# Weights rounded three units ahead before the eviction of the present unit, and norm steps one unit earlier, in a two-block transformer kernel

## The chip, the cores and the metric

The kernel runs on one core of a Trainium2 chip. The metric is the time of one execution on the device in microseconds. Three runs of the kernel before gave 3142.19 (median), 3136.18 and 3153.81 us.

## What is computed

A sequence of 256 tokens with 1024 features passes two blocks of two layers each. Everything is fp32.

The first block, per layer: a projection `x @ w_in` whose parts feed a sliding-window attention, a gated short convolution and a block attention; the three results are projected, weighted with sigmoid gates and summed; then a residual sum with a layer norm, a SwiGLU network and a second residual sum with a layer norm:

```python
x = layer_norm(ALPHA * x + mix, ln1_g[l], ln1_b[l])
ffn = swiglu(x, w_ffn_gate[l], w_ffn_up[l], w_ffn_down[l])   # hidden size 2816
x = layer_norm(ALPHA * x + ffn, ln2_g[l], ln2_b[l])
```

The second block has two streams, the latents `h` (256 tokens, from the first block) and a context `hc` (256 tokens). Each layer modulates them by a vector `mod = silu(c) @ w_ada[l] + b_ada[l]`:

```python
h = h + 0.5 * gt1 * swiglu_2(ada_norm(h, g_ffn1[l], sh1, sc1), w1_ffn1[l], w3_ffn1[l], w2_ffn1[l])
u = ada_norm(h, g_mix[l], sh2, sc2)        # rms_norm(h, g) * (1 + scale) + shift
# convolution, latent attention and Fourier mixing of u @ w_in[l], merged by gates
h = h + gt2 * y
h = h + 0.5 * gt3 * swiglu_2(ada_norm(h, g_ffn2[l], sh3, sc3), w1_ffn2[l], w3_ffn2[l], w2_ffn2[l])
```

and the same for `hc`, except that its last updates in the second layer aren't needed.

## The kernel before, in words

Features lie on the 128 partitions, tokens in the free dimension; `h` holds context in columns 0 to 255 and latents in 256 to 511. All weight matrices are cut into *units*, tiles of up to eight 128x128 blocks (kt blocks, 512 KB where kt is 8), 850 in all, stored one behind the other in the order of use. Every product is computed as three fp32r products: weights and inputs are split into a rounded high part and a remainder, and TensorE adds high x high, high x low and low x high (lines 1767 to 1769; 1711 to 1713 where two units are interleaved). A full unit has 24 such products, on 256 or on 512 columns.

Each unit passes a chain over four slots (`SLOTS = 4`): SP loads it into `raw` (line 434), ACT rounds it into `whi` (`high`, line 521), DVE computes the remainder `wlo` (`low`, line 990), TensorE multiplies, and ACT or DVE takes the result out of one of four PSUM banks (the eviction, `evac`). Semaphores tie the steps: `unit_high_ready`, `unit_low_ready`, and `unit_used`, which TensorE raises at the end of a unit. SP loads unit u+4 when `low(u)` is done; `high(u)` waits for its load and for unit u-4 to be used, since it overwrites that slot. Weights are split three units ahead (`AHEAD = 3`).

Each engine has its own program, written out in order, and runs it in that order. The program goes by stages, named after what is computed: qkv0, bbb0, gate0, merge0, out0, up00, down00, up01 ... for the first block (block number left out, the first digit is the layer), then fup100c, fdown100c, fup100 ... for the second (f1 and f2 are the two SwiGLU networks, a final c means context columns). `stream` runs a stage: for each unit j it calls the eviction of unit j, `high` (on ACT) or `low` (on DVE) of unit j+3, and then, if given, a step of something else, `then(j)`. Where `then` is missing a hardware loop runs over four or twelve units. The stages qkv, bbb, gate, mix, kv and q have loops of their own, in which `high` and `low` already stand in front.

In an up stage (`hidden`) units alternate between gate and up matrix. For even j ACT evicts with SiLU (line 607); for odd j DVE multiplies (line 1166), ACT rounds the product (610) and DVE computes its remainder (1023). In a down stage DVE evicts by adding to the residual (lines 1305, 1308 or 1428).

Beside the up and down stages DVE also computes the modulation vector: one 512 KB tile of `w_ada` after another, loaded through POOL's queue (493), multiplied and summed with `silu(c)` (line 1054). The table `BESIDE` says how many such tiles go with four units of a stage.

The norms of the second block lie beside the stages around them. For one stream a norm has these steps: squares on ACT (638) and their sum on DVE (1223), a sum over features by a small matmul on PE (`by_token`, 1733), the square root on ACT (642, with a table load on each side where SiLU is in use), the reciprocal and a diagonal matrix on DVE (1232, 1177), a matmul with ones that spreads it over the partitions (`spread`, 1752), and then for each of the eight tiles `half_apply` on DVE (1245), `half_shift` on ACT (648) and `half_low` on DVE (1251). A `Follow` record says behind which unit each step stands: the sum, the root, the inverse, the spread, and for each unit the tiles. `DOWN` is used in the down stage whose other stream is just being computed, `UP` in fup200c and fup110c, `INTO` in mix0, `INTO_LAST` in mix1. `seam` runs the two halves of a down stage, with the norm of the first half beside the second.

The layer norms of the first block (`norm1`) stand between stages and TensorE waits for them.

## Time and profile before

| | us |
|---|---|
| median of three runs (lowest, highest) | 3142.19 (3136.18, 3153.81) |
| profiled execution | 3141.47 |
| its span, first to last instruction | 3139.8 |
| TensorE matmuls busy | 2978.0 (95%) |
| VectorE (DVE) busy | 2075.6 (66%) |
| ScalarE (ACT) busy | 1367.1 (44%) |
| mean granted TensorE clock | 0.977 |

The span is nearly the whole execution. Matmuls overlap and the profiler models their ends, so TensorE's busy share is not a share of its peak; the time from the start of one matmul to the start of the next tells its pace. Idle time of DVE and ACT costs nothing where TensorE doesn't wait for them. The clock is given as a share of 2.4 GHz; 0.5 is the lower level, 1.2 GHz.

### The profile page before, as it was taken

How to read it: one execution, taken by the hardware profiler on the slowest of the kernel's cores; microseconds unless marked ns; L12 is line 12 of the kernel's file. 1: busy time of each engine (PE TensorE's matmuls, PEld its weight loads, DVE VectorE, ACT ScalarE, POOL GpSimd, SP SyncE). 2: the span in 40 equal slices, each digit the busy share in tenths (PEclk: the TensorE clock that was granted, in tenths of full speed). 3: DMA queues.
4: the chain of work that ended last, by engine and by line, in shares of the span. 5: the costliest groups of instructions: out<-in, count | busy, mean ns of one | idle time of the engine just before them, and what ended most of it. 6: DMA issues, size and time to landing. Idle time of an engine off the chain costs nothing.

```text
span 3139.8 us, 52114 instructions
## 1 busy us (share of the span) xinstructions
PE 2978.0 (95%) x19700; PEld 2677.8 (85%) x19700; DVE 2075.6 (66%) x3359; ACT 1367.1 (44%) x2222; POOL 76.6 (2%) x149
## 2 busy tenths in 40 slices
PE   8998998998999999999889999999999999889898
PEld 8888998887999988897568888888998889769898
DVE  4657785557777777778843366767767667775655
ACT  4555444454545432354542254222542225654443
POOL 0000000000000000000000000100001000000000
PEclk9999999998999999999999999999999999999999
DMA  6435664434665565551102344544545445215454
GB/s 230 139 104 168 227 233 162 139 104 160 202 211 180 187 215 190 176 177 61 57 29 92 98 168 154 194 156 172 185 145 198 151 147 169 90 54 188 154 186 141
DMA packets 147696, 486.16 MB, mean 155 GB/s; under 512 B 16320, under 2 KB 25792, under 8 KB 147392
## 3 DMA queue, kind: packets, MB, share of 16 engines
q1 hardware_dynamic: 126640, 407.22, 38.5%
q0 software_dynamic: 20880, 76.56, 7.1%
q8 instruction: 115, 1.88, 0.2%
q14 instruction: 61, 0.50, 0.0%
HBM read 482.66 MB, written 1.05 MB: 154 GB/s over the span
## 4 chain that ended last, share of the span: by engine, by line
PE 78%; DVE 11%; ACT 5%; issue 4%; DMA 1%; DVEq 0%; ACTq 0%; SPq 0%; POOLq 0%
PE bank L1767 22%; PE bank L1769 21%; PE bank L1768 21%; DVE wlo L990 4%; ACT whi L521 3%; PE bank L1711 2%; PE bank L1712 2%; PE bank L1713 2%; DVE acc L1515 1%; DMA bbb<-in_w_ada 1%; PE bank L1984 1%; PE bank L1842 1%; DVE bbb L1054 1%; PE aux L1968 1%; DVE big L1245 1%
## 5 line engine op out<-in xcount | busy, mean ns | idle before, releaser
L990 DVE TENSOR_TENSOR wlo<-raw,whi 128x1024 fp32r<-128x1024 f32 (+4 forms) x850 | 948.2, 1116 | 482.1 <-ACT whi L521 479.6
L1767 PE MATMUL bank<-uhi,whi 128*128 128x256 f32 (+1 forms) x4000 | 1250.2, 313 | 16.5 <-DVE wlo L990 9.8
L1768 PE MATMUL bank<-ulo,whi 128*128 128x256 f32 (+1 forms) x4000 | 1237.7, 309 | 0.0
L1769 PE MATMUL bank<-uhi,wlo 128*128 128x256 f32 (+1 forms) x4000 | 1237.6, 309 | 0.0
L521 ACT CAST whi<-raw 128x1024 fp32r<-128x1024 f32 (+4 forms) x850 | 805.9, 961 | 271.1 <-PE bank L1769 170.3
L1767 PEld LDWEIGHTS bank<-uhi,whi 128*128 128x128 f32 x4000 | 757.2, 189 | 79.8 <-issue 22.5
L1768 PEld LDWEIGHTS bank<-ulo,whi 128*128 128x128 f32 x4000 | 757.5, 189 | 44.8 <-issue 0.2
L1769 PEld LDWEIGHTS bank<-uhi,wlo 128*128 128x128 f32 x4000 | 757.3, 189 | 44.6
L1767 PE MATMUL bank<-yhi,whi 128*128 128x256 f32 (+1 forms) x1432 | 444.5, 310 | 21.3 <-DVE wlo L990 14.7
L1768 PE MATMUL bank<-ylo,whi 128*128 128x256 f32 (+1 forms) x1448 | 445.7, 308 | 0.0
L1769 PE MATMUL bank<-yhi,wlo 128*128 128x256 f32 (+1 forms) x1432 | 440.1, 307 | 0.0
L1767 PEld LDWEIGHTS bank<-yhi,whi 128*128 128x128 f32 x1432 | 272.9, 191 | 41.4 <-DVE wlo L990 14.7
L1768 PEld LDWEIGHTS bank<-ylo,whi 128*128 128x128 f32 x1448 | 275.9, 191 | 14.6
L1769 PEld LDWEIGHTS bank<-yhi,wlo 128*128 128x128 f32 x1432 | 272.6, 190 | 14.3
L610 ACT CAST yhi<-pp 128x256 fp32r<-128x256 f32 (+3 forms) x108 | 53.7, 498 | 355.0 <-DVE pp L1166 355.0
L1054 DVE CUSTOM_DVE_ANT_0 acc<-big,cs 128x1024 f32<-128x1024 f32 x128 | 156.4, 1222 | 20.7 <-DMA big<-in_w_ada 18.9
L1428 DVE SCALAR_TENSOR_TENSOR h<-bank,hgt,h 128x256 f32<-128x256 f32 x168 | 77.4, 480 | 100.7 <-PE bank L1769 76.0
L607 ACT ACTIVATE pp<-bank 128x256 f32<-128x256 f32 (+1 forms) x108 | 51.1, 473 | 210.0 <-PE bank L1769 205.9
L1711 PE MATMUL bank<-uhi,whi 128*128 128x256 f32 x288 | 90.0, 312 | 46.4 <-DVE ulo L1023 29.1
L1054 DVE CUSTOM_DVE_ANT_0 acc<-vt,cs 128x1024 f32<-128x1024 f32 x102 | 124.6, 1222 | 2.2
L1166 DVE TENSOR_TENSOR pp<-pp,bank 128x256 f32<-128x256 f32 (+1 forms) x108 | 57.5, 533 | 99.4 <-PE bank L1769 99.3
L960 ACT ACTIVATE pp<-bank,par 128x512 f32<-128x512 f32 (+1 forms) x48 | 27.9, 582 | 198.0 <-PE bank L1769 198.0
(265 smaller groups left out, 2922.2 us busy)
## 6 DMA issues: line engine op xcount, KB each, us to landing
raw<-in_w_stream SPq DMA_DIRECT2D x674, 512.0 KB, 3.4
big<-in_w_ada POOLq DMA_DIRECT2D x64, 512.0 KB, 3.8
vt<-in_w_ada POOLq DMA_DIRECT2D x51, 512.0 KB, 3.7
raw<-in_w_stream SPq DMA_DIRECT2D x80, 256.0 KB, 2.7
raw<-in_w_stream SPq DMA_DIRECT2D x48, 384.0 KB, 3.1
bbb<-in_w_ada POOLq DMA_DIRECT2D x29, 512.0 KB, 3.7
raw<-in_w_stream SPq DMA_DIRECT2D x32, 192.0 KB, 2.3
raw<-in_w_stream SPq DMA_DIRECT2D x16, 128.0 KB, 2.0
```

Of the source, the lines that this page charges most:

```text
L521: sc.copy(whi[:, u % SLOTS, 0:n], raw[:, u % SLOTS, 0:n]).then_inc(s_high, 1)
L610: sc.copy(ht[:, 2 * i + (tile + k), c0:c1], hid(k)[:, c0:c1]).then_inc(s_ahi, 1)
L990: ve.tensor_tensor(wlo[:, u % SLOTS, 0:n], raw[:, u % SLOTS, 0:n], whi[:, u % SLOTS, 0:n].bitcast(F32), ALU.subtract).then_inc(s_low, 1)
L1054: ve.tensor_tensor_reduce(out_, ring(name)[r], cs[:, s, :].rearrange("p (a b) -> p a b", a=out_.shape[1]), 1.0, 0.0, ALU.mult, ALU.add, su ...
L1166: ve.tensor_tensor(hid(k)[:, c0:c1], sg(k)[:, c0:c1], bank(u0, j)[:, c0:c1], ALU.mult).then_inc(read(u0, j), 1)
L1428: ins = ve.scalar_tensor_tensor(h[:, m, cols], bank(u0, j)[:, cols], gate(m, s), h[:, m, cols], ALU.mult, ALU.add)
L1711: te.matmul(out_, whi[:, s, w], hi(k)[:, c0:c1], start=k == 0, stop=False)
L1712: te.matmul(out_, whi[:, s, w], lo(k)[:, c0:c1], start=False, stop=False)
L1713: ins = te.matmul(out_, wlo[:, s, w], hi(k)[:, c0:c1], start=False, stop=k == n - 1)
L1767: te.matmul(out_, whi[:, u % SLOTS, w], hi(k)[:, c0:c1], start=k == 0, stop=False)
L1768: te.matmul(out_, whi[:, u % SLOTS, w], lo(k)[:, c0:c1], start=False, stop=False)
L1769: ins = te.matmul(out_, wlo[:, u % SLOTS, w], hi(k)[:, c0:c1], start=False, stop=k == plan.kt[u] - 1)
```

## The change

Two things change. In `stream` on ACT and DVE, `high` and `low` of unit j+3 now stand in front of the eviction of unit j instead of behind it, in the loop as in the written-out parts. And three `Follow` records get other numbers: in `UP` and `INTO` the sum and the root stand behind unit 2 instead of 3 and the spread behind unit 4 instead of 5; in `UP` the inverse stands behind unit 3 instead of 4 and the tiles begin behind unit 4 instead of 5, one per unit; in `INTO_LAST` the inverse moves from 2 to 3 and the tiles from units 4 to 7 (two each) to units 5 to 7 (two, three, three). `DOWN` is as it was.

```diff
-UP = Follow(3, 3, 4, 5, {5: [0], 6: [1], 7: [2], 8: [3], 9: [4], 10: [5], 11: [6, 7]})
-INTO = Follow(3, 3, 3, 5, {5: [0], 6: [1], 7: [2], 8: [3], 9: [4], 10: [5], 11: [6, 7]})
-INTO_LAST = Follow(2, 2, 2, 4, {4: [0, 1], 5: [2, 3], 6: [4, 5], 7: [6, 7]})
+UP = Follow(2, 2, 3, 4, {4: [0], 5: [1], 6: [2], 7: [3], 8: [4], 9: [5], 10: [6], 11: [7]})
+INTO = Follow(2, 2, 3, 4, {5: [0], 6: [1], 7: [2], 8: [3], 9: [4], 10: [5], 11: [6, 7]})
+INTO_LAST = Follow(2, 2, 3, 4, {5: [0, 1], 6: [2, 3, 4], 7: [5, 6, 7]})
...
                 if then is not None:
                     for j in range(n):
+                        high(u0 + j + AHEAD)
                         evac(j % per, j // per)
-                        high(u0 + j + AHEAD)
                         then(j)
                     return
 
                 def body(i):
                     for j in range(per):
+                        high(u0 + j + AHEAD, i, per)
                         evac(j, i)
-                        high(u0 + j + AHEAD, i, per)
 
                 repeat(act, iters - 1, body, tallies)
                 for j in range(per):
+                    high(u0 + n - per + j + AHEAD)
                     evac(j, iters - 1)
-                    high(u0 + n - per + j + AHEAD)
...
```

The same three moves are made with `low` in `stream` on DVE.

The first place is DVE behind the loop of stage up00. L990 is the remainder of a weight unit, L1054 the sum over a tile of `w_ada` (its second row reads the sum), L1166 the product of an odd unit and L1023 its remainder. Before:

```order
L201 COMPARE_AND_BRANCH
L1054 ISA bbb,ada_sums<-bbb,cs 128x1024 [waits ada_sums_ready,ada_modulation_ready,ada_landed0]
L1054 ISA ada_sums 128x1
L990 TENSOR_TENSOR wlo<-raw,whi 128x1024 [waits unit_high_ready]
L1166 TENSOR_TENSOR lg<-lg,bank 128x256 [waits unit_used,bank_read2]
L1023 TENSOR_TENSOR ylo<-lg,yhi 128x256 [waits act_high_ready]
L990 TENSOR_TENSOR wlo<-raw,whi 128x1024 [waits unit_high_ready]
```

and now:

```order
L201 COMPARE_AND_BRANCH
L990 TENSOR_TENSOR wlo<-raw,whi 128x1024 [waits unit_high_ready]
L1054 ISA bbb,ada_sums<-bbb,cs 128x1024 [waits ada_sums_ready,ada_modulation_ready,ada_landed0]
L1054 ISA ada_sums 128x1
L990 TENSOR_TENSOR wlo<-raw,whi 128x1024 [waits unit_high_ready]
L1166 TENSOR_TENSOR lg<-lg,bank 128x256 [waits unit_used,bank_read2]
L1023 TENSOR_TENSOR ylo<-lg,yhi 128x256 [waits act_high_ready]
L990 TENSOR_TENSOR wlo<-raw,whi 128x1024 [waits unit_high_ready]
```

L990 has moved in front of L1054 with its wait for the tile of `w_ada`, and in front of L1166 and L1023; the order among the others is as it was.

The second place is DVE behind the sixth unit (j = 5) of stage fdown202, a seam with a norm. L1428 is the eviction, L1223 adds a square, L1245 applies the norm to a tile, L1251 computes a tile's remainder. Before:

```order
L1428 SCALAR_TENSOR_TENSOR h<-bank,hgt,h 128x256 [waits unit_used]
L990 TENSOR_TENSOR wlo<-raw,whi 128x1024 [waits unit_high_ready]
L1223 TENSOR_TENSOR big<-big 128x256 [waits norm_squares_ready,dve_step]
L1245 SCALAR_TENSOR_TENSOR big<-h,scl,aux 128x256 x2
L1251 SCALAR_TENSOR_TENSOR ulo<-big,mod,uhi 128x256 [waits half_high_ready]
```

and now:

```order
L990 TENSOR_TENSOR wlo<-raw,whi 128x1024 [waits unit_high_ready]
L1428 SCALAR_TENSOR_TENSOR h<-bank,hgt,h 128x256 [waits unit_used]
L1223 TENSOR_TENSOR big<-big 128x256 [waits norm_squares_ready,dve_step]
L1245 SCALAR_TENSOR_TENSOR big<-h,scl,aux 128x256 x2
L1251 SCALAR_TENSOR_TENSOR ulo<-big,mod,uhi 128x256 [waits half_high_ready]
```

L1428 has moved from the front of the row to the place between L990 and L1223.

The third place is ACT in stage fup110c, behind the second unit. L521 is the rounding of a weight unit, L607 SiLU of an even unit, L610 the rounding of an odd unit's product, L782 and L785 the table loads around the square root L642, L648 the shift of a norm tile. Before:

```order
L521 CAST whi<-raw 128x1024 [waits unit_used,unit_landed1]
L610 CAST yhi<-pp 128x256 [waits bank_read3]
L521 CAST whi<-raw 128x1024 [waits unit_used,unit_landed2]
L782 ACT_TABLE_LOAD
L642 ACTIVATE tok<-aux,cst 128x2 [waits sum_ready]
L785 ACT_TABLE_LOAD
L607 ACTIVATE pp<-bank 128x256 [waits unit_used]
L521 CAST whi<-raw 128x1024 [waits unit_used,unit_landed3]
L610 CAST yhi<-pp 128x256 [waits bank_read1]
L521 CAST whi<-raw 128x1024 [waits unit_used,unit_landed0]
L648 ACTIVATE uhi<-big,mod 128x256 [waits half_applied]
```

and now:

```order
L521 CAST whi<-raw 128x1024 [waits unit_used,unit_landed1]
L607 ACTIVATE pp<-bank 128x256 [waits unit_used]
L782 ACT_TABLE_LOAD
L642 ACTIVATE tok<-aux,cst 128x2 [waits sum_ready]
L785 ACT_TABLE_LOAD
L521 CAST whi<-raw 128x1024 [waits unit_used,unit_landed2]
L610 CAST yhi<-pp 128x256 [waits bank_read3]
L521 CAST whi<-raw 128x1024 [waits unit_used,unit_landed3]
L607 ACTIVATE pp<-bank 128x256 [waits unit_used]
L648 ACTIVATE uhi<-big,mod 128x256 [waits half_applied]
L521 CAST whi<-raw 128x1024 [waits unit_used,unit_landed0]
```

Each L521 stands in front of its L607 or L610. The square root with its two table loads now stands behind the SiLU of unit 2 and in front of the rounding that goes with unit 3, and the first L648 follows one unit sooner.

## Rows read from the trace of the kernel before

**Rows 1.** Page, part 1: busy time, share of the span, instructions.

```profile
PE 2978.0 (95%) x19700; PEld 2677.8 (85%) x19700; DVE 2075.6 (66%) x3359; ACT 1367.1 (44%) x2222; POOL 76.6 (2%) x149
```

**Rows 2.** Page, part 5: L990; idle time and its releaser come last.

```profile
L990 DVE TENSOR_TENSOR wlo<-raw,whi 128x1024 fp32r<-128x1024 f32 (+4 forms) x850 | 948.2, 1116 | 482.1 <-ACT whi L521 479.6
```

**Rows 3.** Waits by total: sum us, times, longest us.

```profile
PE bank L1711 <- DVE ulo L1023: 29.1, 6, 10.7
```

**Rows 4.** Windows: us; PE, PEld, DVE, ACT, POOL busy (count); clock, DMA share, GB/s.

```profile
1226.00:1315.60 89.60, 89.60 (x385) 72.05 (x384) 66.28 (x98) 23.31 (x30) 8.41 (x16) 1.00 0.53 190
297.90:340.30 42.40, 40.94 (x339) 40.08 (x338) 30.27 (x44) 19.07 (x30) 1.58 (x3) 1.00 0.57 198
363.10:410.30 47.20, 46.24 (x385) 45.62 (x385) 39.81 (x62) 19.55 (x30) 3.16 (x6) 1.00 0.66 233
787.10:828.10 41.00, 39.99 (x335) 39.53 (x334) 30.83 (x46) 18.68 (x29) 1.71 (x4) 1.00 0.60 207
850.90:898.50 47.60, 46.41 (x388) 45.81 (x389) 32.88 (x50) 21.11 (x32) 1.58 (x3) 1.00 0.57 198
1058.50:1101.70 43.20, 40.87 (x338) 40.05 (x338) 30.40 (x46) 19.03 (x30) 1.58 (x3) 1.00 0.58 196
```

**Rows 5.** Timeline of DVE in stage fup100: start us, busy us, instruction, [idle before].

```profile
1067.97 1.23 DVE L990 TENSOR_TENSOR wlo<-raw,whi 128x1024 fp32r<-128x1024 f32 x1 [0.31 <-ACT whi L521]
1071.36 1.22 DVE L1054 CUSTOM_DVE_ANT_0 acc<-big,cs 128x1024 f32<-128x1024 f32 x1 [2.16 <-DMA big<-in_w_ada]
...
1072.51 1.22 DVE L990 TENSOR_TENSOR wlo<-raw,whi 128x1024 fp32r<-128x1024 f32 x1
...
1085.55 0.08 DVE L1054 DVE_READ_ACCUMULATOR2_ANT ada_sums<- 128x1 f32 x1
1085.55 1.22 DVE L990 TENSOR_TENSOR wlo<-raw,whi 128x1024 fp32r<-128x1024 f32 x1
```

**Rows 6.** Timeline of DVE at the end of stage fdown202.

```profile
2252.94 1.23 DVE L990 TENSOR_TENSOR wlo<-raw,whi 128x1024 fp32r<-128x1024 f32 x1 [0.73 <-ACT whi L521]
2254.09 0.42 DVE L1223 TENSOR_TENSOR big<-big 128x256 f32<-128x256 f32 x1
2254.42 0.47 DVE L1245 SCALAR_TENSOR_TENSOR big<-h,scl,aux 128x256 f32<-128x256 f32 x1
2255.61 0.48 DVE L1428 SCALAR_TENSOR_TENSOR h<-bank,hgt,h 128x256 f32<-128x256 f32 x1
2256.42 1.22 DVE L990 TENSOR_TENSOR wlo<-raw,whi 128x1024 fp32r<-128x1024 f32 x1 [0.33 <-ACT whi L521]
```

**Rows 7.** Timeline of ACT, the same stretch, and one table load in fup110c.

```profile
2254.93 0.51 ACT L648 ACTIVATE uhi<-big,mod 128x256 fp32r<-128x256 f32 x1 [1.70 <-DVE big L1245]
2255.35 1.04 ACT L521 CAST whi<-raw 128x1024 fp32r<-128x1024 f32 x1
...
2269.08 1.28 ACT L782 ACT_TABLE_LOAD   x1
```

**Rows 8.** Timeline of DVE in the second half of stage fup110c.

```profile
2291.84 0.42 DVE L1166 TENSOR_TENSOR pp<-pp,bank 128x256 f32<-128x256 f32 x1
2292.73 0.43 DVE L1023 TENSOR_TENSOR ylo<-pp,yhi 128x256 fp32r<-128x256 f32 x1 [0.47 <-ACT yhi L610]
```

**Rows 9.** Timeline of PE in fup110c: the ones-matmul and its wait.

```profile
2275.11 1.22 PE L1752 MATMUL aux<-pp,cst 128*128 128x256 f32 x2 [2.89 <-DVE pp L1177]
```

**Rows 10.** Windows of the same seventh unit in fup110c and in fup200c.

```profile
2273.50:2281.40 7.90, 6.29 (x28) 6.11 (x29) 3.90 (x7) 1.88 (x4) 0.00 (x0) 0.57 0.38 135
1887.00:1893.60 6.60, 3.70 (x30) 3.53 (x29) 4.10 (x7) 2.76 (x5) 0.00 (x0) 1.00 0.35 132
```

**Rows 11.** Timeline of DVE at the end of stage out0.

```profile
277.58 1.22 DVE L990 TENSOR_TENSOR wlo<-raw,whi 128x1024 fp32r<-128x1024 f32 x1
```

**Rows 12.** Timeline of DVE in stage merge0, one period apart.

```profile
241.78 0.69 DVE L990 TENSOR_TENSOR wlo<-raw,whi 128x512 fp32r<-128x512 f32 x1
246.60 0.69 DVE L990 TENSOR_TENSOR wlo<-raw,whi 128x512 fp32r<-128x512 f32 x1
```

6 lines of the change are left out of this document (3 added, 3 removed).

## Prediction, written before the changed kernel ran

> **What bounds the kernel now.** I read the page's busy shares first, then its costliest groups, then the waits, then windows over single stages, and last the timelines of DVE and ACT at the seams between stages. TensorE is busy for 95% of the span, 2978 of 3139.8 us [rows 1], so an edit that only reorders ACT and DVE can win at most the roughly 160 us in which TensorE stands, and what it stretches. The largest idle time elsewhere is DVE's, 479.6 us before L990, the remainder of a weight unit, waiting for L521, the rounding on ACT [rows 2]. That total says nothing by itself: the question is where L990 or a norm step is the last thing TensorE waits for.
>
> A stage that loses nothing gives the measure. In fup102 16 units of 24 products each on 512 columns take 89.6 us [rows 4], 0.117 us per 256 columns, so a full unit on 256 columns needs 2.81 us. Against that: up00 takes 42.4 us for 14 units (39.4 needed), up01 47.2 for 16 (45.0), up10 41.0 for 14, up11 47.6 for 16, fup100 43.2 for 14 [rows 4]. The losses are 3.0, 2.2, 1.6, 2.6 and 3.8 us, 13.2 together. All stages on 512 columns stand like fup102 and cannot gain. The other losses sit at seams, where TensorE waits for normalized tiles (29.1 us in six waits for L1023 alone [rows 3]) and for the small ones-matmul of a norm [rows 9].
>
> **The change part by part.** No instruction is added or removed; the DMAs are the same, in the same order on SP's and POOL's queues. Since SP issues the load of unit u+4 when L990 of unit u is done, loads start earlier wherever L990 does, without more bytes.
>
> A. *Rounding and remainder ahead of the eviction, in the middle of a stage.* Unit j+3's L521 needs only that unit j-1 is used, while the eviction of unit j needs unit j itself. So each L990 moves ahead of one eviction and, in the stages with modulation work, of one L1054. In fup100 DVE waits 2.16 us for a modulation tile in front of L1054, and L990, behind it in the queue, comes at 1072.51; the next such point is at 1085.55 [rows 5]. That is 13.0 us for four units for which TensorE needs 11.3, so DVE's queue, stretched by the transfer, is the slower one, and it stays so: the change shortens no period, it puts one L990 more ahead of each stall. Worked through for up00, L990 comes 0.9 to 3.5 us earlier and takes away about 1.8 of the 3.0 us. For the three stages with one tile per four units (3.0+1.6+3.8 = 8.4) I take 5.0. In up01 and up11 there are two tiles per four units and DVE has no DMA wait but too much work: the lead with which the stage begins is used up at its end. L990 of every other unit moves ahead of a multiplication, a wait, a remainder and an L1054, some 2.6 us (0.42 + 0.47 + 0.43 + 1.22, durations as in [rows 5, 8]), which is more than each of these losses: I take 4.5 of 4.8. With up02 and up12 (half a microsecond) A gives 10.0; bounds 3 (only the starts gain) and 14 (all of it).
>
> B. *Ends of stages.* After the last unit of out0 L990, 1.22 us [rows 11], stands between the last residual sum and the centring that DVE does next. It moves into the time in which TensorE computes that unit. The centring must still wait for the ones-matmul, so only 0.35 us is won, three times (up00, qkv1, up10): 1.0. Before fup210 the same instruction stands ahead of the last square sum: 0.9. At the ends of bm0 and bm1 it stands in front of the eight remainders of u: 1.1 each. Sum 4.1, bounds 2 and 6.
>
> C. *merge0 and merge1.* L990 recurs after 4.82 us for three units [rows 12] that TensorE needs 4.2 for; DVE's own chain of three remainders, three products, two sums, a wait for ACT and one more remainder is the bound, and the cycle is the same in both orders. Only the start and the one stall at the second gating are displaced: 1.0 each, 2.0; bounds 0 and 4.
>
> D. *The seams with a norm (fdown100c, fdown102, bout0, fdown202, fdown112c).* Here the edit works against itself. ACT and DVE hand work to each other: L521, L990 1.07 us later, L1223 1.15 later, L1245 0.33 later, L648 on ACT 0.51 later, and 0.42 later the next L521 [rows 6, 7]; 3.48 us with one tile, more than the 2.81 of TensorE. L1428, the eviction (0.48 busy, 0.40 to the next start, since an instruction begins 0.08 before its forerunner ends), stands at 2255.61, in the part in which DVE would otherwise wait for ACT [rows 6]. It is free there. After the change it stands between L990 and L1223, inside the ring. Five rounds cost 2.0 us; the first tile comes 1.0 to 1.15 earlier, since L990 no longer sits between its eviction and L1245. Net the last tile comes 1.0 us later, and TensorE already waits for it. Loss 4 x 1.0 + 0.85 = 4.9; bounds 0 and 7.
>
> E. *UP, one unit earlier (fup200c, fup110c).* The square root and its two table loads of 1.28 us [rows 7] move from behind unit 3 to behind unit 2, the inverse to unit 3, the ones-matmul to behind unit 4. It gets there 2.8 us sooner, but its operand only 1.5 to 2.2 us sooner, because the inverse now stands behind an eviction, its copy and its remainder, so its wait grows from 2.89 [rows 9] to about 3.5 us. The tiles start one unit earlier and need one round fewer at the end; but on odd units L1245 now stands behind L1166 and L1023, 0.89 us apart [rows 8], which before ran beside ACT's rounding. A pair of units goes from 7.2 to 7.55 us. All told each first pair of fup200l and fup110l ends 0.35 us later beyond D: loss 0.7.
> The granted clock matters here. After the same wait the seventh unit's window has a clock of 0.57 in fup110c, 1.00 in fup200c; TensorE is busy for 6.29 us in the one and 3.70 in the other [rows 10], 2.6 us for half the clock (1.2 instead of 2.4 GHz). I leave one such stretch in two, as before: 0, bounds +2.6 and -2.6.
> The Trainium skill, "TensorE: Matmul & The Clock Gate", section "Part 1: The HAM clock gate", says that the gate's timing is not tied to the kernel, so the same program meets it differently from run to run; these rows agree, one wait of two having paid. By that rule the value taken stands; by the rows alone both waits, now longer, might pay, which is the third rival's price.
>
> F. *INTO and INTO_LAST.* In mix0 TensorE doesn't wait for the steps that move: 0. In mix1 the last step now holds three tiles instead of two and the one before it three as well; each tile costs about 0.4 on ACT and 0.8 on DVE: the context pair ends 1.2 us later. Bounds 0 and 1.7.
>
> Sum: 10.0 + 4.1 + 2.0 - 4.9 - 0.7 - 1.2 = 9.3 us less. The profiled execution took 3141.5 us (span 3139.8 and 1.7 around it), the median of the runs is 3142.2, so both stand together: 3132 in the profile, 3133 as a median.
>
> **The rivals.** *The seams don't pay and the stalls go entirely (faster).* If the eviction in D lies beside something after all and one more L990 ahead absorbs every modulation stall: 13.7 + 4.1 + 4 + 2.6 for the half clock = 24, so 3118. For it: leads at full lie near 6 us where DVE isn't late. Against it: 13.0 against 11.3 us per four units [rows 5].
> *Nothing measurable.* TensorE at 95% [rows 1] and gains at one end given back at the next: a unit ready earlier only waits in its slot. A at its lower bound of 3 with B 4.1 and C 2 against D to F 6.8 gives 2.3: 3140.
> *The seams win (slower).* The handshake of D with L1428 inside is the one place where TensorE surely waits. If A stays at 3 and B at 2, while the waits for the ones-matmul both fall into half clock (2.6 more) and D reaches 7: 3 + 2 - 7 - 2.6 - 0.7 - 1.7 = 7 slower, 3149. It decides from the point where a round costs more than 3.9 us. For it: the ring is already 3.48 us against 2.81. Against: A is five stages of clear, late L990.
>
> **How the numbers follow.** Forecast 3133: 0.45. Faster rival 3118: 0.25. Nothing: 0.18. Slower: 0.12. A measurement of this kernel can tell about 0.5%, 15.7 us. Below 3126.5 lies the faster rival and a fifth of the forecast: 0.34. Above 3157.9 lies the tail of the slower one: 0.07. The rest, 0.59, is within. The bounds of A to F reach from 3112 to 3150; the range 3115 to 3146 leaves one case in five out. The forecast's own range is 3125 to 3139.
>
> **What would show it.** A: in the windows of up00, up01, up10, up11 and fup100, shifted to where these stages then lie, 1 us or less lost in the two-tile stages, 1 to 2 in the others; L1054's DMA wait still there, L990 ahead of it. B: L1183 starts some 0.3 us closer to the last L1305. D: at the end of fdown202 L1428 between L990 and L1223, rounds of 3.9 us, TensorE's waits for L1023 larger by 1 us each. E: the wait before L1752 in fup110c about 3.5 us. The prediction is wrong if a round at the seams is no longer than 3.5 us, if the up stages keep their losses, or if the share of half clock (mean clock 0.977) moves by more than 0.003.

## The result and the profile after

The changed kernel takes 3150.32 us (median of 16 runs, 3145.22 to 3157.07) against 3143.31 (16 runs) of the kernel before on the same chip: ratio 1.0028, 95% interval 1.0018 to 1.0037. The prediction was 3133, range 3115 to 3146. By the ratio it is slower by about 8.8 us (the medians differ by 7.0) where 9.3 us less was forecast.

TensorE does the same work for the same time; what changed is where the others wait. Page, parts 1 and 5, after:

```profile
PE 2978.5 (95%) x19700; PEld 2678.1 (85%) x19700; DVE 2077.7 (66%) x3359; ACT 1374.2 (44%) x2222; POOL 76.6 (2%) x149
...
L990 DVE TENSOR_TENSOR wlo<-raw,whi 128x1024 fp32r<-128x1024 f32 (+4 forms) x850 | 948.4, 1117 | 565.7 <-ACT whi L521 558.9
```

DVE's wait for ACT before L990 rose from 479.6 [rows 2] to 558.9 us. Again the total alone says nothing. The windows of the five up stages do (the same units as in [rows 4], where they now lie: up00, up01, up10, up11, fup100):

```profile
295.70:336.10 40.40, 40.16 (x336) 39.68 (x335) 28.71 (x43) 17.01 (x27) 1.58 (x3) 1.00 0.61 208
361.40:406.40 45.00, 45.00 (x386) 45.00 (x386) 37.28 (x58) 18.93 (x29) 3.17 (x6) 1.00 0.66 232
783.30:823.10 39.80, 39.80 (x336) 39.32 (x334) 28.18 (x43) 16.64 (x26) 1.58 (x3) 1.00 0.62 211
848.70:894.20 45.50, 45.50 (x388) 45.50 (x389) 30.73 (x47) 19.79 (x29) 1.58 (x3) 1.00 0.57 197
1061.10:1104.30 43.20, 40.69 (x336) 39.87 (x334) 28.93 (x43) 17.59 (x27) 1.58 (x3) 1.00 0.57 195
```

In these windows the change did much of what it should: 42.4, 47.2, 41.0, 47.6 and 43.2 us became 40.4, 45.0, 39.8, 45.5 and 43.2, 7.5 us less, and TensorE stands still in up01 no more; fup100 alone gained nothing. But what comes behind the last unit of each stage is another matter. DVE at the end of up00, in the kernel before (start us, busy us, instruction, idle before it):

```profile
333.97 1.23 DVE L1054 CUSTOM_DVE_ANT_0 bbb<-bbb,cs 128x1024 f32<-128x1024 f32 x1
335.12 1.22 DVE L990 TENSOR_TENSOR wlo<-raw,whi 128x1024 fp32r<-128x1024 f32 x1
...
342.40 0.43 DVE L1023 TENSOR_TENSOR ylo<-lg,yhi 128x256 fp32r<-128x256 f32 x1 [0.47 <-ACT yhi L610]
```

and in the changed one, with TensorE's waits behind it:

```profile
331.50 1.22 DVE L990 TENSOR_TENSOR wlo<-raw,whi 128x1024 fp32r<-128x1024 f32 x1 [0.33 <-ACT whi L521]
334.59 1.23 DVE L1054 CUSTOM_DVE_ANT_0 bbb<-bbb,cs 128x1024 f32<-128x1024 f32 x1 [1.86 <-DMA bbb<-in_w_ada]
335.74 1.22 DVE L990 TENSOR_TENSOR wlo<-raw,whi 128x1024 fp32r<-128x1024 f32 x1
...
341.00 1.22 DVE L990 TENSOR_TENSOR wlo<-raw,whi 128x1024 fp32r<-128x1024 f32 x1
342.14 0.41 DVE L1166 TENSOR_TENSOR lg<-lg,bank 128x256 f32<-128x256 f32 x1
343.02 0.42 DVE L1023 TENSOR_TENSOR ylo<-lg,yhi 128x256 fp32r<-128x256 f32 x1 [0.47 <-ACT yhi L610]
```

```profile
337.01 0.38 PE L1711 MATMUL bank<-yhi,whi 128*128 128x256 f32 x1 [0.88 <-DVE wlo L990]
...
343.50 0.39 PE L1711 MATMUL bank<-yhi,whi 128*128 128x256 f32 x1 [0.75 <-DVE ylo L1023]
```

L1023 in DVE's last row makes the last of the tiles that the down stage multiplies. TensorE ended up00 at 340.3 before and at 336.1 after, 4.2 us earlier; this tile was ready at 342.8 before and is ready at 343.4 after, 0.6 us later, since one more L990 stands ahead of it and L1054 now waits 1.86 us for its transfer. The interleaved first two units of the down stage need all tiles and wait. They also wait for their own weights: 0.88 us for L990 in the row at 337.01. In the kernel before, the profile shows no wait of TensorE for DVE in down00, down01, down10, down11 and fdown100; after the change it waits there for 3.5 us in all for L990 and for 3.8 us for the last L1023 of the up stage. What the up stage won is waited for in the down stage.

The lengths of whole stages give a full account. Each runs from one moment to the next at which TensorE signals the last unit of a stage (the semaphore events of the trace; these numbers are in no row). After minus before, us:

| stages | up | down | pair |
|---|---|---|---|
| up00, down00 | -2.2 | +2.5 | +0.3 |
| up10, down10 | -1.0 | +2.8 | +1.8 |
| up11, down11 | -2.1 | +1.3 | -0.8 |
| fup100, fdown100 | +0.3 | +2.3 | +2.6 |
| up01, down01 | -2.1 | +0.9 | -1.2 |
| up02, down02 | -0.8 | -0.8 | -1.5 |
| up12, down12 | +2.3 | +4.2 | +6.5 |
| merge and out, both layers | | | -1.9 |
| mix0, fup200, fup110, mix1 | | | +7.8 |

The first four pairs have one buffer for the tiles of `w_ada` (`BESIDE` 1; call them the single-buffer pairs), the next two have two. The rest, -6.7, is spread: bout0c, bout1 and fup210 -3.5, fdown102c and fdown202c -1.4, and stretches at half clock that lie elsewhere. Such stretches are in these numbers too: the four norm stages of the last row hold 3.4 us more at half clock than before, worth about half of that.

up12 stands in no term of my sum. It has norm steps between its units. DVE and ACT there after:

```profile
957.71 0.48 DVE L1245 SCALAR_TENSOR_TENSOR big<-h,scl,aux 128x256 f32<-128x256 f32 x1
959.48 0.96 DVE L990 TENSOR_TENSOR wlo<-raw,whi 128x768 fp32r<-128x768 f32 x1 [1.30 <-ACT whi L521]
960.36 0.41 DVE L1166 TENSOR_TENSOR lg<-lg,bank 128x256 f32<-128x256 f32 x1
961.24 0.43 DVE L1023 TENSOR_TENSOR ylo<-lg,yhi 128x256 fp32r<-128x256 f32 x1 [0.47 <-ACT yhi L610]
```

```profile
958.22 0.51 ACT L648 ACTIVATE uhi<-big,mod 128x256 fp32r<-128x256 f32 x1 [2.28 <-DVE big L1245]
958.64 0.81 ACT L521 CAST whi<-raw 128x768 fp32r<-128x768 f32 x1
960.81 0.40 ACT L610 CAST yhi<-lg 128x256 fp32r<-128x256 f32 x1 [1.35 <-DVE lg L1166]
```

L648 waits 2.28 us for DVE's L1245; the rounding L521 stands behind it; DVE's L990 waits 1.30 us for that rounding, and the eviction L1166 and L1023 behind L990 wait too. It is the ring of term D with an eviction caught in it. TensorE, which had ended up12 at 954.9, stands in down12 for the last tile, and the granted clock falls to its lower level. The wait, then the window after, and that of the kernel before:

```profile
961.72 0.58 PE L1711 MATMUL bank<-yhi,whi 128*128 128x256 f32 x1 [2.97 <-DVE ylo L1023]
```

```profile
961.00:965.00 4.00, 3.28 (x16) 3.28 (x17) 3.38 (x7) 2.51 (x4) 0.00 (x0) 0.57 0.53 146
```

```profile
961.00:965.00 4.00, 4.00 (x36) 4.00 (x36) 3.93 (x8) 1.36 (x2) 0.00 (x0) 1.00 0.75 202
```

16 products instead of 36 in 4 us.

The seams look as predicted. DVE and ACT at the end of fdown202 after, against [rows 6, 7]:

```profile
2262.44 1.23 DVE L990 TENSOR_TENSOR wlo<-raw,whi 128x1024 fp32r<-128x1024 f32 x1 [0.72 <-ACT whi L521]
2263.59 0.48 DVE L1428 SCALAR_TENSOR_TENSOR h<-bank,hgt,h 128x256 f32<-128x256 f32 x1
2263.98 0.41 DVE L1223 TENSOR_TENSOR big<-big 128x256 f32<-128x256 f32 x1
2264.31 0.47 DVE L1245 SCALAR_TENSOR_TENSOR big<-h,scl,aux 128x256 f32<-128x256 f32 x1
```

```profile
2260.97 0.51 ACT L648 ACTIVATE uhi<-big,mod 128x256 fp32r<-128x256 f32 x1 [2.09 <-DVE big L1245]
...
2264.82 0.51 ACT L648 ACTIVATE uhi<-big,mod 128x256 fp32r<-128x256 f32 x1 [2.09 <-DVE big L1245]
```

L648 comes again after 3.85 us (3.9 predicted), and L648's wait rose from 1.70 to 2.09, by L1428's 0.39. TensorE's waits at three of the four seams grew by 0.8 us (from 2.03 to 2.13 for L990, and a new one of 0.71 for L1251), where 1 us each was predicted. The wait ahead of the ones-matmul in fup110c, 2.89 before [rows 9], was predicted at 3.5:

```profile
2279.49 1.22 PE L1752 MATMUL aux<-pp,cst 128*128 128x256 f32 x2 [3.60 <-DVE pp L1177]
```

### The profile page after: what moved, and what is told of

It is laid out like the page before. It is cut to its first block, busy times and chain, and to the rows that moved or that the text cites. A ratio compares the mean times of both kernels' runs of the same rounds, so it can differ in the third digit from the quotient of the medians.

```text
span 3147.3 us, 52114 instructions
## 1 busy us (share of the span) xinstructions
PE 2978.5 (95%) x19700; PEld 2678.1 (85%) x19700; DVE 2077.7 (66%) x3359; ACT 1374.2 (44%) x2222; POOL 76.6 (2%) x149
## 4 chain that ended last, share of the span: by engine, by line
PE 71%; DVE 13%; ACT 6%; issue 6%; DMA 3%; DVEq 0%; ACTq 0%; POOLq 0%; SPq 0%; POOL 0%
PE bank L1767 20%; PE bank L1769 20%; PE bank L1768 20%; DVE wlo L990 4%; ACT whi L521 3%; PE bank L1711 2%; PE bank L1712 2%; PE bank L1713 2%; DVE acc L1515 2%; DMA bbb<-in_w_ada 2%; DVE bbb L1054 1%; PE bank L1984 1%; DVE ylo L1023 1%; DVE big L1245 1%; DMA big<-in_w_ada 1%
## 5 line engine op out<-in xcount | busy, mean ns | idle before, releaser
L990 DVE TENSOR_TENSOR wlo<-raw,whi 128x1024 fp32r<-128x1024 f32 (+4 forms) x850 | 948.4, 1117 | 565.7 <-ACT whi L521 558.9
L521 ACT CAST whi<-raw 128x1024 fp32r<-128x1024 f32 (+4 forms) x850 | 810.6, 961 | 321.4 <-PE bank L1769 227.5
L1767 PEld LDWEIGHTS bank<-uhi,whi 128*128 128x128 f32 x4000 | 756.7, 189 | 75.2 <-issue 24.2
L610 ACT CAST yhi<-pp 128x256 fp32r<-128x256 f32 (+3 forms) x108 | 53.8, 498 | 370.4 <-DVE pp L1166 370.4
L1054 DVE CUSTOM_DVE_ANT_0 acc<-big,cs 128x1024 f32<-128x1024 f32 x128 | 156.3, 1221 | 26.4 <-DMA big<-in_w_ada 24.6
L1711 PE MATMUL bank<-uhi,whi 128*128 128x256 f32 x288 | 91.4, 317 | 50.7 <-DVE ulo L1023 26.9
L607 ACT ACTIVATE pp<-bank 128x256 f32<-128x256 f32 (+1 forms) x108 | 51.0, 473 | 179.6 <-PE bank L1769 177.9
L1054 DVE CUSTOM_DVE_ANT_0 acc<-vt,cs 128x1024 f32<-128x1024 f32 x102 | 124.6, 1221 | 2.2
L1428 DVE SCALAR_TENSOR_TENSOR h<-bank,hgt,h 128x256 f32<-128x256 f32 x168 | 77.2, 479 | 70.4 <-PE bank L1769 48.2
L1166 DVE TENSOR_TENSOR pp<-pp,bank 128x256 f32<-128x256 f32 (+1 forms) x108 | 57.5, 532 | 95.1 <-PE bank L1769 95.0
L1711 PEld LDWEIGHTS bank<-uhi,whi 128*128 128x128 f32 x288 | 62.8, 218 | 56.6 <-issue 31.7
```

What stands on the lines that cost most here:

```text
L521: sc.copy(whi[:, u % SLOTS, 0:n], raw[:, u % SLOTS, 0:n]).then_inc(s_high, 1)
L990: ve.tensor_tensor(wlo[:, u % SLOTS, 0:n], raw[:, u % SLOTS, 0:n], whi[:, u % SLOTS, 0:n].bitcast(F32), ALU.subtract).then_inc(s_low, 1)
L1054: ve.tensor_tensor_reduce(out_, ring(name)[r], cs[:, s, :].rearrange("p (a b) -> p a b", a=out_.shape[1]), 1.0, 0.0, ALU.mult, ALU.add, su ...
L1166: ve.tensor_tensor(hid(k)[:, c0:c1], sg(k)[:, c0:c1], bank(u0, j)[:, c0:c1], ALU.mult).then_inc(read(u0, j), 1)
L1428: ins = ve.scalar_tensor_tensor(h[:, m, cols], bank(u0, j)[:, cols], gate(m, s), h[:, m, cols], ALU.mult, ALU.add)
L1711: te.matmul(out_, whi[:, s, w], hi(k)[:, c0:c1], start=k == 0, stop=False)
```

## The experiments

Stage lengths of one profile scatter: with the same order throughout the four single-buffer pairs they took 318.3 us together in one profile (after) and 327.3 in another (x11). So they are read over many profiles here. The table has each kernel's groups of stages: the four single-buffer pairs, the two pairs with two buffers, up12 with down12, the four norm stages, and the ratio to the kernel before. "ahead" is the changed order, "back" the order before. The sets of runs were taken on different chips; each ratio is against the kernel before in the same set.

| kernel | one buffer | two | up12 | norms | ratio (95%) |
|---|---|---|---|---|---|
| before | 314.4 | 122.8 | 52.0 | 323.0 | 1 |
| after | 318.3 | 120.1 | 58.5 | 330.8 | 1.0028 (1.0018, 1.0037) |
| after_again | 323.7 | 120.1 | 59.7 | 330.2 | 1.0022 (1.0008, 1.0036) |
| x1: back, new tables | 317.0 | 122.7 | 51.8 | 324.5 | 1.0007 (0.9997, 1.0017) |
| x2: ahead, old tables | 325.0 | 120.1 | 58.5 | 325.5 | 1.0000 (0.9986, 1.0014) |
| x3: last four of up back | 337.4 | 121.9 | 58.0 | 331.8 | 1.0074 (1.0055, 1.0092) |
| x4: x3, old tables, norms back | 338.1 | 121.9 | 51.8 | 326.6 | 1.0032 (1.0019, 1.0046) |
| x11: norms back | 327.3 | 120.4 | 51.8 | 327.4 | 1.0006 (0.9991, 1.0022) |
| y1: norms, one buffer back, old tables | 316.2 | 120.2 | 52.0 | 324.2 | 0.9970 (0.9958, 0.9982) |
| y2: y1 with new tables | 325.4 | 120.2 | 52.0 | 325.9 | 0.9971 (0.9955, 0.9986) |
| z1: ahead in one buffer only | 332.4 | 122.8 | 52.0 | 326.7 | 1.0006 (0.9993, 1.0019) |
| e1: last unit of up back | 326.2 | 121.7 | 59.9 | 332.2 | 1.0031 (1.0018, 1.0045) |
| e2: up12 back | 324.1 | 120.4 | 52.1 | 330.0 | 1.0012 (0.9997, 1.0027) |
| y4: e1, merge's last unit too, old tables, norms back | 324.2 | 121.5 | 51.8 | 325.5 | 0.9997 (0.9984, 1.0010) |
| y3: mixed order, norms back, old tables | 312.0 | 123.1 | 51.8 | 322.2 | 0.9952 (0.9935, 0.9969) |
| y6: mixed in one buffer, ahead in others, norms back, old tables | 310.2 | 120.6 | 51.9 | 325.7 | 0.9954 (0.9936, 0.9972) |
| x9: after, short transfer | 306.1 | 120.2 | 57.6 | 332.5 | 0.9959 (0.9946, 0.9972) |
| x10: before, short transfer | 303.3 | 122.9 | 52.0 | 327.9 | 0.9964 (0.9952, 0.9976) |
| x5: after, short sum | 311.0 | 119.6 | 55.0 | 329.2 | 0.9941 (0.9919, 0.9963) |
| x6: before, short sum | 315.0 | 118.3 | 50.7 | 329.2 | 0.9945 (0.9923, 0.9968) |

**Tables alone, order alone (x1, x2).** x1 is the kernel before with the three new `Follow` lines, x2 the changed kernel with the three old ones.

> The kernel before with only the three new Follow tables; the order of weights and evictions stays as it was. Theory 1 (the loss comes from the order ahead: evictions late at the ends of the up stages, and L1428's norm multiplication inside the weight ring at the seams): the tables alone move the time by between -1 and +2.5 us, so 3142 to 3146 beside a kernel before of about 3143. The five stages that end in a Follow of the UP or INTO kind change by under 1 us each. Theory 2 (the tables are the cause, because the norm steps stand earlier beside the first units of qkv and mix): +5 to +7 us, 3148 to 3150, nearly all of it in mix0, fup200, fup110 and mix1.

> The changed kernel with the Follow tables of the kernel before: only the order of weights and evictions on ACT and DVE is new. Theory 1: +4 to +7 us over the kernel before (3147 to 3150); the up stages shorter by 1 to 2 us each and the down stages after them longer by 1 to 3 us each, as in the changed kernel. Theory 2 (tables): within 1 us of the kernel before or faster, 3137 to 3144, with mix0, fup200, fup110 and mix1 as before.

x1's time came out as theory 1 had it, though fup110 (-1.5) and mix1 (+1.3) moved by more than 1 us. x2 missed theory 1: its time equals that of the kernel before, which is theory 2's number. Of the stage pattern the down stages (+0.8 to +3.3) and up12 with down12 (+6.5) came as expected, but up00, up10 and fup100 were 0.9 to 1.1 us longer and not shorter. The clock may hide a part of the cost: over its runs x2's mean granted clock was 0.9785 against 0.976 for the kernel before, which comes to some 15 us less at the lower level. Neither half alone costs what both together do: in the norm stages 324.5 and 325.5 apart, and 330.8 together. The kernels with both old parts (before, x4, y1, y3, y4, y6, z1) have 322.2 to 326.7 there, 324.8 on average; over that the order adds 0.7 (x2, one profile), the tables 1.1 (x1, y2, x11), and both 6.2 (after twice, x3, e1, e2). TensorE's wait ahead of the ones-matmul, in fup200c and fup110c, shows where both meet, in the kernels that leave no work out: 2.76 to 2.90 us with both old parts, 2.56 to 2.62 with the new tables alone, 2.45 and 2.06 with the order alone, but 3.03 to 3.67 with both. The two ones-matmuls behind the wait took 1.10 to 1.22 us together, wholly or mostly at the lower clock, in all ten cases with both, and 0.70 in all eight with one new part.

**Order back in the last four units of the up stages (x3, x4).** The same on DVE with `low`; `late` is true in `hidden`. A stage with norm steps between its units, up12 among them, goes by the `then` branch and is left alone.

```diff
                 for j in range(per):
-                    high(u0 + n - per + j + AHEAD)
+                    if not late:
+                        high(u0 + n - per + j + AHEAD)
                     evac(j, iters - 1)
+                    if late:
+                        high(u0 + n - per + j + AHEAD)
```

> The changed kernel with one piece undone: in the written-out last iteration (four units) of every hidden (up) stage without interleaved norm steps, ACT and DVE evict first again and round three units ahead afterwards. Theory 1 (the order ahead makes the last evictions of an up stage late, and the first units of the down stage wait for those very ylo tiles): 6 to 8 us faster than the changed kernel (3142 to 3145); down00, down10, down11, down12 and fdown100 come back to within 0.7 us of the kernel before, and half or more of what the up stages gained stays. Rival (the weights asked for earlier meet the modulation tiles' transfers, so that L1054's sum waits longer for its DMA, wherever it stands): under 2 us faster, the down stages as long as in the changed kernel. Rival (what the up stages gain is only shifted, TensorE being held by DVE over the pair of stages): the down stages come back, and the up stages lose their gain by as much, the time stays within 1.5 us.

> The changed kernel with before's tables, before's order in the stages with interleaved norm steps (the seams, L1428), and before's order in the last four units of every hidden stage; the order ahead stays in all loops, in the merges, downs and outs. Theory 1: the cost of the seams (mix0, fup200, fup110, mix1: +8.5 us together in the changed kernel) and of the late ylo tiles is gone, and of the gains in the up stages, merges and bouts 5 to 9 us are left: 3134 to 3139, 4 to 9 us under the kernel before. Rival (the gain is only shifted between an up stage and its down stage): within 2 us of the kernel before.

Both missed badly. down00, down10, down11 and fdown100 did come back to within 0.3 us of the kernel before, as theory 1 said, but up00, up10, up11 and fup100 grew by 6.5 to 8.3 us over the changed kernel in x3, and by 5.1 to 8.3 in x4. down12, which x3's expectation counts among the stages that come back, stayed at +4.2 over before, since the edit doesn't reach up12. The edit has a flaw of its own: where the order changes from ahead to back, two evictions follow each other without a weight tile between, and the second is L1054 waiting for its transfer. DVE in up00 of x3 (L993, L1060 and L1029 are the other kernels' L990, L1054 and L1023):

```profile
331.39 1.22 DVE L993 TENSOR_TENSOR wlo<-raw,whi 128x1024 fp32r<-128x1024 f32 x1
332.53 0.41 DVE L1172 TENSOR_TENSOR lg<-lg,bank 128x256 f32<-128x256 f32 x1
333.65 0.42 DVE L1029 TENSOR_TENSOR ylo<-lg,yhi 128x256 f32 x1 [0.71 <-ACT yhi L613]
334.00 0.15 DVE L1065 TENSOR_TENSOR mod<-ada_sums,par 128x2 f32 x1
338.03 1.23 DVE L1060 CUSTOM_DVE_ANT_0 bbb<-bbb,cs 128x1024 f32<-128x1024 f32 x1 [3.88 <-DMA bbb<-in_w_ada]
339.18 1.22 DVE L993 TENSOR_TENSOR wlo<-raw,whi 128x1024 fp32r<-128x1024 f32 x1
```

No L993 starts between 331.39 and 339.18, 7.8 us, in which TensorE needs 2.8 units. So it matters what stands behind the wait for the transfer.

**Is it the transfer? (x9, x10)** In both kernels, which leave most of the modulation sum out of the result:

```diff
-                    pool.dma_start(to, src.rearrange(...)).then_inc(s_ada_land[r], 16)
+                    src = src.rearrange(...)
+                    pool.dma_start(to[:, 0:1, 0:64], src[:, 0:1, 0:64]).then_inc(s_ada_land[r], 16)
...
-                    ve.tensor_tensor_reduce(out_, ring(name)[r], cs[:, s, :] ...
+                    ve.tensor_tensor_reduce(out_ ..., ring(name)[r][:, 0, 0:64].unsqueeze(2)
+                                            .to_broadcast([P, 64, 16]), cs[:, s, :] ...
```

> The changed kernel, with each modulation tile's transfer cut from 1024 to 64 columns (32 KB instead of 512 KB); L1054's sum runs over the same number of elements, which it reads from those 64 columns, so DVE's work stays and most of the modulation sum is left out of the result. To be compared with the kernel before with the same cut. Theory 2 (the order ahead puts the weight transfers in front of the single modulation tile's, whose landing DVE waits for in up00, up10, up11, up12, fup100): the gap between the two cut kernels in those stages and their down stages closes to under 1 us a pair, and with it 6 to 10 us of the difference; this one is 10 to 25 us faster than the changed kernel. Theory 1 (DVE's queue itself is late, transfers don't matter): the down stages still lose 1 to 3 us each against the cut kernel before, and the total difference stays +5 to +9 us.

> The kernel before with the same cut of the modulation tiles' transfers (64 of 1024 columns loaded, the sum as long as before over those 64 columns; most of the modulation sum is left out of the result). Theory 2 (waits for the modulation tile cost the changed kernel more): 8 to 20 us faster than the kernel before, within 2 us of the changed kernel with the cut. Theory 1: the same or up to 15 us faster than before, and 5 to 9 us faster than the changed kernel with the cut.

Theory 2, here that of the transfers, came true for the down stages: down00, down01 and down11 differ by under 0.4 us between the two, down10 and fdown100 by 0.4 and 0.5, and TensorE waits for L990 in none of them. Only down01, which has two buffers, keeps a wait of 0.6 us for the last L1023. The totals came out equal as well, 3135.4 us each. But not every pair closed: fup100 with fdown100 is still 2.2 us longer in x9, and up12 with down12, which theory 2 also named, 5.6; the norm stages are 4.6 longer. So a part of the equal total is the clock: x10's profile has 20 us more at half clock than x9's, and over all runs their mean clocks are 0.9754 and 0.977. What the pair of runs shows is that without the long transfers the down stages lose nothing to the order. Both kernels also move less data, so the load on the DMA engines changed with the wait.

**Is it DVE's work? (x5, x6)** L1054 over 64 of 1024 columns, transfers as they are.

```diff
-                    ve.tensor_tensor_reduce(out_, ring(name)[r], ...
+                    ve.tensor_tensor_reduce(out_[:, 0:1, 0:64], ring(name)[r][:, 0:1, 0:64], ...
```

> The changed kernel with L1054's sum over 64 of the 1024 columns, so that DVE's 256 modulation sums cost a fraction of their 1.22 us each, while every transfer stays as it is; most of the modulation sum is left out of the result. Theory 2 (transfers collide): the modulation tile is asked for earlier in DVE's slack, the landings stay 0.5 to 0.8 us longer than in the kernel before with the same cut, but DVE has room and TensorE loses little by it: pairs of up and down stages within 1.5 us of each other between the two cut kernels. Theory 1 (DVE's own work is too long with the order ahead): the pairs' gap closes as well. Both kernels get faster by 5 to 25 us. What tells the theories apart is the landing time alone: if it is equal in both cut kernels, the order of DVE's work sets it, and not the order in which the two queues ask.

> The kernel before with the same cut of L1054's sum (64 of 1024 columns; most of the modulation sum is left out of the result). 5 to 20 us faster than the kernel before; with either theory the changed kernel with this cut lies within 4 us of it, since the merges and the stage ends gain 4 us and the seams lose 8.

In x5 down00 and down10 are still 1.8 and 2.0 us longer than in x6, although DVE's sums cost nearly nothing; down11, down01 and fdown100 differ by 0.0, 0.2 and 0.5. TensorE's waits in x5 tell which part is which: it still waits for L990, 1.1 us in down00 and 1.3 in down10, but nowhere in these five stages for the last L1023. So the late weights come from the wait for the transfer, which the cut of the sum leaves; the late tile goes with either cut, so DVE's work has a share in it. The totals, 0.9941 and 0.9945, close here as they did with the short transfer, so they don't tell the two causes apart. Nor does the landing time (median 5.2 us in x5, 4.6 in x6), by which x5's expectation meant to decide: in kernels with before's order it is 3.7 to 4.8 us, with the changed order 4.4 to 5.2, and the groups overlap. That the order makes transfers slower (theory 2's reason) isn't shown.

**The norm stages back (x11), single buffers back as well (y1, y2), single buffers ahead alone (z1).** x11 has before's order in `stream`'s `then` branch. y1 has the old tables besides, and passes, in `hidden` on both engines,

```diff
+stream(..., late=plan.ada.get(name, (0, 0))[1] == 1)
```

where `late` sets before's order in the loop and behind it; y2 is y1 with the new tables. z1 has before's tables, and its order everywhere but in those stages.

> The changed kernel, new tables included, with before's order only in the stages that have norm steps between their units (the `then` branch). Term D of the prediction (+6.8 to +7.8 us for mix0, fup200, fup110 and mix1): 5 to 9 us faster than the changed kernel, 3141 to 3146 beside its 3150, and 1.0000 to 1.0010 of the kernel before. Rival (the seams' difference is luck of the granted clock, 3.4 us at half clock in mix0 and in fup200): within 3 us of the changed kernel.

> Before's tables, before's order in the stages with norm steps between their units and in the whole of the stages that keep a single modulation buffer (up00, up10, up11, up12, fup100, fdown100); the order ahead everywhere else (merges, outs, downs, up01 and up02 with two buffers, bm, bout, fup210). If the loss sits in the single-buffer stages and the seams, what is left is gains: merge with out -1.0 us twice, up01 with down01 -1.2, up02 with down02 -1.5, fdown102c, fdown202c -0.7 each, bout0 and bout1 -1 each, fup210 -0.6, less up to 1 us at each of five changes of order: 3 to 8 us faster than the kernel before (ratio 0.9975 to 0.9990). If the gains are only shifted: within 2 us of before.

> The version that beat the kernel before (order ahead, but before's order in the single-buffer hidden stages and in the stages with norm steps between their units), with the new Follow tables instead of before's. Terms E and F of the prediction (norm steps one unit earlier are worth -1.9 us together): 3134 to 3142, within 3 us of the version with the old tables, ratio 0.996 to 0.998 of before. Rival (the new tables cost by themselves, as the order with the old tables was 0.28% faster than the changed kernel): 4 to 8 us slower than with the old tables, ratio 0.9985 to 1.0.

> The kernel before (its tables, its order) with the order ahead in the five hidden stages up00, up10, up11, up12 and fup100 alone, which keep a single modulation buffer. Theory 2 (the order ahead puts more weight transfers beside the single modulation tile's): +3 to +8 us over the kernel before (ratio 1.001 to 1.0025), the modulation tiles of the bbb kind land in a median of 4.3 us or more instead of 3.7, and down00, down10, down12, fdown100 are 1 to 3 us longer. Rival (the changed kernel loses elsewhere, the stages with one buffer only by luck of the clock): within 1.5 us of before, landing as before.

(fdown100 isn't a hidden stage: in y1 and y2 it kept the order ahead, and in z1 the order back, unlike what y1's expectation says; up12 goes by the `then` branch, so z1 leaves it alone.) x11 came out as expected, y1 slightly better. y1 is the first version faster than the kernel before; y2 equals it, so with the norm stages back the tables are worth nothing either way. z1 is a half: its four down stages lose 3.3, 2.9, 1.2 and 8.4 us, as expected or more, but the time, 1.0006, is the rival's. The 8.4 of fdown100 holds the same flaw as x3: the order changes from ahead to back in front of it, DVE's sum waits 4.02 us for its transfer with no weight tile for 8.8 us, and TensorE waits 3.8 us for one. Its profile, at 3163.3 us, is slower than its median of 3154.7, so the stage times overstate. By times alone the single-buffer stages cost 0.35% between x11 and y2 and 0.06% in z1, with errors of some 0.2% and 0.13%: a cost, of a size that isn't settled.

**Only the last unit back (e1, y4), mixed order (y3), and the changed kernel again.** e1 takes the order back for unit 3 of the last four alone. y4 does it for the merges' last unit too, with the norm stages and the tables as before. y3 has, in every hidden stage without norm steps, in the loop and behind it, the order ahead at even units and back at odd ones:

```diff
                     for j in range(per):
+                        if j not in back:
+                            high(u0 + j + AHEAD, i, per)
                         evac(j, i)
-                        high(u0 + j + AHEAD, i, per)
+                        if j in back:
+                            high(u0 + j + AHEAD, i, per)
...
-                stream(u0, plan.count[name], 4, evac, then=then)
+                stream(u0, plan.count[name], 4, evac, then=then, back=(1, 3))
```

on both engines, with the norm stages and the tables as before and the merges' last unit back as in y4. Call this the mixed order.

> The changed kernel with one unit undone in each hidden stage: for the stage's last unit (and no other) ACT and DVE evict first and round the weights three units ahead afterwards. Refined theory 1 (the last ylo or y2lo tile of a stage is late because a rounding, itself held by L1054's wait for its transfer, stands in front of its eviction on DVE): down00, down01, down10, down11 and fdown100 come back to within 0.7 us of the kernel before, down12 too where TensorE's clock isn't lost; the up stages stay as in the changed kernel; in all 5 to 9 us faster than the changed kernel, ratio 1.0000 to 1.0012 of before. Rival (the loss builds up over the whole of a stage with a single modulation buffer): the down stages come back by under half, and the time stays within 3 us of the changed kernel.

> As the run before in this list, and also before's order for the last unit of the merge stages, before's Follow tables, and before's order in the stages with norm steps between their units. Refined theory 1: the gains in the up stages and merges stay and nothing is handed back: ratio 0.9955 to 0.9970 of the kernel before, as fast as or faster than the version with before's order in the single-buffer stages (0.9970). Rival: 0.998 or more, since the single-buffer stages still lose.

> As the run before, but in every hidden stage the order goes by the unit's place in its pair: at the even unit, which on DVE has only L1054's sum and on ACT the Silu, the rounding comes first; at the odd unit, which has the eviction L1166 and L1023, the eviction comes first. So a weight tile never stands behind L1054's wait, and an eviction never behind a weight tile that TensorE doesn't need yet. Refined theory 1: ratio 0.995 to 0.997. Rival (order within the pair is without effect; the transfer's wait is the same): 0.997 to 0.999.

> The changed kernel once more, beside the others on one chip: ratio 1.0020 to 1.0037 of before. Its down00, down10 and fdown100 are again 1.5 us or more over the kernel before; the stages that hold a stretch at half clock may differ by one or two such stretches of 3.4 us, so 1.7 to 3.4 us each.

e1 refutes the refined theory: it is no faster than the changed kernel. down00, down01 and down11 are longer still (+3.3, +1.8, +3.0 over before); down10 and fdown100 came down to +1.4 and +0.3. TensorE's waits show why: in these five stages it waits no more for the last ylo tile, but 7.1 us in all for L990 (3.5 in the changed kernel). Moving one L990 from in front of the last eviction to behind it made a weight of the down stage late instead. y3, 3134.39 us, is with y6 the fastest of the kernels that compute everything. DVE at the end of up00 in y3 (L996, L1066, L1035):

```profile
329.60 2.36 DVE L996 TENSOR_TENSOR wlo<-raw,whi 128x1024 fp32r<-128x1024 f32 x2 [0.33 <-ACT whi L521]
333.18 1.23 DVE L1066 CUSTOM_DVE_ANT_0 bbb<-bbb,cs 128x1024 f32<-128x1024 f32 x1 [1.21 <-DMA bbb<-in_w_ada]
...
340.48 0.42 DVE L1035 TENSOR_TENSOR ylo<-lg,yhi 128x256 fp32r<-128x256 f32 x1 [0.47 <-ACT yhi L616]
```

Two weight tiles stand ahead of the wait, and one fewer ahead of the last L1035. Summed over the kernel, L1054's waits for tiles in `bbb` are, after and in y3:

```profile
DVE bbb L1054 <- DMA bbb<-in_w_ada: 16.6, 10, 3.2
```

```profile
DVE bbb L1066 <- DMA bbb<-in_w_ada: 10.3, 9, 1.4
```

In the kernels with the order ahead this sum is 16.6 to 25.2, with before's order 11.2 to 22.0, so it is low in y3 but hardly lower than in the kernel before (11.2). Not all of y3's gain is the mixed order's: y1, with the norm stages and the single buffers back, already stands at 0.9970 (0.9958 to 0.9982), and y3's 0.9952 (0.9935 to 0.9969) can't be told from it with certainty by times alone. y4, 0.9997, missed like e1 and came out as its rival had it. after_again confirms the result of the changed kernel.

**up12 (e2), and the order chosen by buffers (y6).** e2 keeps before's order where `u0 == U["up12"]`; y6 has the mixed order in single-buffer stages and the order ahead in the other hidden ones; the merges' last unit, back in y3, is ahead in y6.

> The changed kernel with before's order in up12 alone (12 units with L1245, L648 and L1251 between them). Theory (in up12 the roundings and the norm steps hold each other: DVE's L990 waits for ACT's L521, that stands behind L648, that waits for DVE's L1245): up12 and down12 come back to within 0.5 us of the kernel before, the stretch at half clock near 961 us goes, all other stages stay; 5 to 7 us faster than the changed kernel, ratio 1.0000 to 1.0015. Rival (the half clock there is luck): under 2.5 us faster, ratio 1.0015 to 1.0030.

> Before's tables, before's order in the stages with norm steps between their units, the mixed order (rounding first at even units, eviction first at odd ones) in the hidden stages with one modulation buffer, and the order ahead everywhere else, so also in up01, up02 and the later hidden stages. Against the version with the mixed order in all hidden stages: up01 with down01 -1.2, up02 with down02 -1.5, fdown102c and fdown202c -0.6 to -0.8 each, so 3 to 4 us faster, ratio 0.9935 to 0.9955 of before. Rival (DVE's queue is the bound in up01 and up02, what TensorE gains there it waits for in the down stage): the same as that version, 0.9945 to 0.9965.

In e2 up12 and down12 are back at 52.1 us, and its window at that place is at full clock:

```profile
962.00:966.00 4.00, 3.80 (x30) 3.40 (x29) 3.21 (x8) 3.24 (x6) 0.00 (x0) 1.00 0.45 136
```

The pair is 58.0 to 59.9 us in the five profiles with the order ahead there and 51.8 to 52.1 in the eleven with it back (those with less work left aside), without exception: it isn't luck. The time, 1.0012 (0.9997 to 1.0027), fits 1.0028 and 1.0022 less 0.2%, but its interval reaches both the theory's and the rival's range; the stage lengths decide. y6 has 120.6 us in the two-buffer pairs where y3 has 123.1, as expected, but their times, 3133.49 and 3134.39, can't be told apart. Either is faster than the kernel before by some 15 us.

## Why the prediction was wrong

**A failed (10.0 us to be gained).** The step was: L990 comes earlier by one eviction and one L1054, so TensorE's stalls in the up stages are gained. In the up stages themselves this held for the most part (7.5 us in five windows, 9.5 forecast for them), though not in fup100. The sum ended there: it has no term for what the later evictions and weights do to the down stage behind. The sentence "it stays so: the change shortens no period" was right too, and I didn't draw its consequence. With every L990 one place further ahead, the last ylo tile came late, which the down stage's first two units need, and after the longer waits for a transfer the first weights of that stage came late as well. down00, down01, down10, down11 and fdown100 lost 9.8 us together; TensorE, which had no wait for DVE there before, waited 3.8 us for the tile and 3.5 for the weights. Net, the six pairs of A gave +1.2 us in the profile shown. The four single-buffer pairs took 325.1 us on average over six profiles with the order ahead (after, after_again, x2, x11, z1, e2), 318.2 over four with it back (before, x1, y1, y2) and 311.1 over the two with the mixed order. The groups overlap (318.3 to 332.4 against 314.4 to 325.4), so the size of the cost stays open. Only the two-buffer pairs gained, 2.2 to 2.7 us in every profile with the order ahead throughout them and nothing left out. x9 against x10 and x5 against x6, in one profile each, show that the late weights come from the wait for the transfer; the late tile has a share of DVE's own work. Why the mixed order is better than the old one, and by how much, is argued from its rows, not taken apart by a run.

A also took up11 for a stage with two tiles per four units and no wait for a transfer. `BESIDE` gives it one, and DVE waits there for 5.5 us in three waits before the change.

**The list of the seams was short.** D's mechanism, the ring with an eviction inside, was right, but it also acts in up12, which has no L1428: there the eviction is L1166 and L1023. It costs 6.5 us with the half clock that follows; e2 takes them back. This is the largest loss at one place, and reading which `stream` calls pass `then` would have found it.

**D, E and F** (4.9 + 0.7 + 1.2 = 6.8 forecast) measured 7.8 in the profile, 6.2 over all kernels. The sum is near, in part by luck, since the split was wrong: the order alone, which is D, costs 0.7 and the tables 1.1, only both together 6.2. E had the longer wait before the ones-matmul right (3.66 and 3.60 us, 3.5 forecast), but took one stretch at half clock in two; after the change both waits have one. With the new tables alone that wait is shorter than before.

**B and C** (4.1 and 2.0) came near: merges with outs -1.9; bout0c, bout1 and fup210 -3.5 together, of which bout0c's -1.8 goes with one stretch less at half clock. qkv1, of which I expected 0.35, shows +1.4 with one more stretch at half clock.

**The rival that ended slower** had D and the clock at 7 and A at 3, with 0.12. What happened is near its sum, but by other terms: A at nothing and up12, which it didn't name, in D's place. That is luck. Nor did any of the three signs that were to show the prediction wrong come up: rounds at the seams were over 3.5 us, the up stages lost less, and the mean clock of the profile was 0.976 against 0.977. None of them watched the stages behind the up stages. And the bounds of A to F add up to some 3116 to 3149 us, not 3112 to 3150.
